# Gated-delta loop of a hybrid decoder trunk: eight heads a chunk at a time, against two groups of four heads half a chunk apart

## Chip, cores, metric

One core of one Trainium2 chip. The metric is device time in microseconds (us) of one launch; before: 3519.69 us, median of 3 runs (3516.3 to 3522.31). A difference of 0.2% is about what a measurement of this kernel can tell from none.

## What is computed

Two layers over 1024 tokens of width 1024, all in float32: layer 0 mixes with gated linear attention and an RG-LRU, layer 1 with a gated DeltaNet of 8 heads (key and value width 128); each layer then attends to 256 memory tokens and applies a squared-ReLU MLP. The change touches the gated DeltaNet's loop alone:

```python
L = jnp.exp(jnp.where(incl, gcum[..., :, None] - gcum[..., None, :], -jnp.inf))
M = jnp.where(strict, jnp.einsum('bhnid,bhnjd->bhnij', kb, kc) * L, 0.0)      # kb = k * beta
IM = M + jnp.eye(CHUNK, dtype=F32)
sol = lax.linalg.triangular_solve(IM, rhs, left_side=True, lower=True, unit_diagonal=True)
Aqk = jnp.where(incl, jnp.einsum('bhnid,bhnjd->bhnij', qc, kc) * L, 0.0)
def step(S, inp):                                       # one chunk, all heads
    v_new = un - jnp.einsum('bhcd,bhdv->bhcv', wn, S)
    o = jnp.einsum('bhcd,bhdv->bhcv', qn * jnp.exp(gn)[..., None], S) + jnp.einsum('bhij,bhjv->bhiv', an, v_new)
    S = S * jnp.exp(glast)[..., None, None] + jnp.einsum('bhcd,bhcv->bhdv', kn * jnp.exp(glast[..., None] - gn)[..., None], v_new)
    return S, o
```

q and k are divided by their l2 norms first; o goes through an RMS norm and is multiplied by a gate (silu(z)).

## The kernel before, in words

The program is written engine by engine; every engine has its own list in program order, and semaphores join them. Nothing is reordered by a planner inside the stage: the order is the order of the calls. Most of the kernel is projections (L1899 and L1915: each weight is split in two parts, three matmuls of 128x512 for one product), with weights streamed by SyncE.

The stage at issue works on 8 chunks of 128 tokens, 8 heads each, data of a chunk in units of 128x1024 (8 heads side by side, 4 heads in each of two PSUM banks). For chunk c+1 it **prepares**, for chunk c it **finishes**, and `both(c)` (one loop round) holds both; `prepare(0)` stands ahead of the loop, `finish(7)` behind it, among the first projections of the output (`out1`).

On TensorE, one round is, in this order:

- `state_keys` (ks, L2224: key times state), `start` (grow, L2234: the cumulated gate sent to all rows by 2 matmuls with ones; kt, L1953: keys transposed; nrm, L2241: squares of q and k summed by 16 matmuls with a column of ones), `new_values` (vn, L2224: inverse times right side), `keys_values` (knt and vt, L1953), `output_state` (o, L2267 and L2268; su, L2224), `matrices` (g and qk, L2224; z, L2285: seeds of the inverse).
- `inverse`: six levels. A level has, for each half k of the heads, `products` (q, L2299, at the last level L2302), 2 transposes of the inverse so far (t, L2334), then `updates` (x, L2313, at the last level L2316), all on 64x64 tiles of the array, 32 columns each. Between products and updates ScalarE copies both results to SBUF (L999 and L1003); after the updates VectorE merges them into the inverse (L1778), and the next level's products wait for it. The halves alternate. The output's transposes (ot, L1953) stand ahead of level 2.

A float32 matmul shows as two records in the trace, a transpose as one.

ScalarE also squares q and k (L958, L960), takes the norms' power (L962, L963), copies vn and knt (L967, L978), computes the decays' exponentials (L971 to L976), squares the output (L983) and issues the loads of q, k, v and the gate (L944, 4 a chunk). VectorE does the products of whole units: 128x1024 TENSOR_TENSORs L1695 to L1793. GpSimd does three products a chunk (L480, L482, L485).

Of the kernel before, what the change touches and what calls it, by code (L numbers as in the profile page):

```python
# [17 lines left out]
F32 = mybir.dt.float32  # L18
# [169 lines left out]
def build(nc, xT, memT, wstream, lru_w, gk_w2, pvec_in, consts_in, masks_in, outT):  # L188
# [4 lines left out]
    with ExitStack() as ctx:  # L193
# [79 lines left out]
        def every(ap, n):  # L273
# [43 lines left out]
        loaded = [sem(f"loaded_{k}") for k in "qkvz"]  # L317
# [3 lines left out]
        inv = range(LEVELS - 1)  # L321

        ppe = Steps(sem("gdn_prep_pe"), "grow kt nrm knt vt g qk z " +
                    " ".join(f"q{n}0 t{n}0 q{n}1 t{n}1 x{n}0 x{n}1" for n in inv))
        fpe = Steps(sem("gdn_fin_pe"), "ks vn o su ot")
        pact = Steps(sem("gdn_prep_act"), "sqk sqq rk eg L LT sc knt " +
                     " ".join(f"q{n}0 t{n}0 q{n}1 t{n}1" for n in inv) + " zd")
        fact = Steps(sem("gdn_fin_act"), "vn osq ro hi")
        ppool = Steps(sem("gdn_prep_pool"), "L qg kd")
        pdve = Steps(sem("gdn_prep_dve"), "dg m kn vb mn z beg at " +  # L330
                     " ".join(f"z{n}{k}" for n in inv for k in range(2)))
        fdve = Steps(sem("gdn_fin_dve"), "r o1 s ss o2 res lo")
# [19 lines left out]
        def in_lin(first, *shape):  # L352
            n = 1
            for k in shape:
# [19 lines left out]
        gs = {name: small[:, 128 + 8 * k:128 + 8 * k + n] for name, k, n in  # L374
              (("rkq", 0, 16), ("dec", 2, 8), ("gd", 3, 8), ("egl", 4, 8), ("gl", 5, 8), ("egt", 6, 8), ("g", 7, 8),
               ("ro", 8, 8), ("oss", 9, 8), ("nb", 10, 8), ("bt", 11, 8), ("beg", 12, 8), ("rqs", 13, 8), ("egs", 14, 8))}
# [10 lines left out]
        own = small[:, 248:312]  # L387
        Qc = unit(14)[:, 0:256].rearrange("p (t m n) -> p t m n", t=2, m=GDN_H // 2)
        Qt = unit(14)[:, 0:256].rearrange("p (m n) -> p m n", m=GDN_H // 2)
# [6 lines left out]
        def gdn_chunks(link, prepare, finish, both, per):  # L396

            prepare(0)
            link.loop(NCH - 2, per, lambda c: both(c, True))
            both(NCH - 2, False)  # L400
            finish(NCH - 1)
# [18 lines left out]
        def _(sp):  # L420
# [9 lines left out]
            for layer in range(2):  # L430
                n1 = plan.at[f"mlp{layer}.1"][0]
                for n in range(n, n1):
                    if n == plan.at["out0"][0] + 3:
                        sp.wait_ge(gpe.sem, gpe.at("tr", NCH - 1))
                    if n == plan.at["out1"][0] + 3:
                        sp.wait_ge(fpe.sem, fpe.at("su", NCH - 1))
# [17 lines left out]
        def _(pool):  # L454
# [22 lines left out]
            def gdn(p):  # L477
# [21 lines left out]
            with pool.Fori(0, NCH) as p:  # L499
                gdn(p)  # L500
# [3 lines left out]
        def _(eng):  # L504
# [378 lines left out]
            def mixer1():  # L883
# [63 lines left out]
                def loads(p):  # L947
# [3 lines left out]
                    for kind in (1, 0, 2):  # L951
                        load(kind, p)
# [1514 lines left out]
```

## Time and profile before

| what | before |
| --- | --- |
| median of 3 runs | 3519.69 us (3516.3 to 3522.31) |
| the profiled execution's own time | 3515.1 us |
| its span, first to last instruction | 3513.3 us |
| mean granted TensorE clock | 0.942 |
| TensorE busy | 3300.2 us, 94% of the span |
| VectorE, ScalarE, GpSimd busy | 1633.0, 1065.3, 155.2 us |
| DMA | 189.10 MB, mean 54 GB/s |

Busy time says little by itself: an engine that waits for a result between two short instructions is idle for a short time each, and TensorE is busy twice as long for the same work when its granted clock is 0.5 (1.2 GHz) and not 1.0 (2.4 GHz). Where the stage is bound has to be read from its own stretch.

### The profile page before, as it was taken

What the parts mean: (1) busy time and instruction counts of PE and PEld (TensorE: products, weight loads), DVE (VectorE), ACT (ScalarE), POOL (GpSimd) and SP (SyncE); (2) the same over time, 40 slices, a digit from 0 to 9 for tenths busy, and PEclk for the clock granted to TensorE, in tenths of its full rate; (3) what the DMA queues carried; (4) which work ended last, traced back from release to release, by engine and by line L of the source; (5) the groups of instructions that cost most, each with busy time, mean ns of one, the idle gap of its engine ahead of it and who ended that gap; (6) DMA issues with size and microseconds to landing.
All of it is one profiled execution on the core that took longest, in us unless ns stands there. A gap on an engine that the chain in (4) does not pass through costs nothing.

```text
span 3513.3 us, 45268 instructions
## 1 busy us (share of the span) xinstructions
PE 3300.2 (94%) x17926; PEld 2686.5 (76%) x17926; DVE 1633.0 (46%) x2171; ACT 1065.3 (30%) x1615; POOL 155.2 (4%) x270
## 2 busy tenths in 40 slices
PE   7996699989999999999999888899998999999997
PEld 6685588767788888877887677778876778888886
DVE  6264556436333333367555444544643543333335
ACT  3332344225222222233111333333432422222222
POOL 0005400000000000000000101100000000000000
PEclk9998899999999999999999677769999999999998
DMA  3010131101111111112222111113110111111112
GB/s 118 30 48 19 54 120 37 42 21 46 45 47 49 47 49 47 49 38 96 96 96 93 49 46 42 30 31 101 62 36 12 49 49 48 48 48 48 48 48 72
DMA packets 80223, 189.10 MB, mean 54 GB/s; under 512 B 5728, under 2 KB 38768, under 8 KB 79600
## 3 DMA queue, kind: packets, MB, share of 16 engines
q1 hardware_dynamic: 40320, 141.91, 12.4%
q10 hardware_dynamic: 39792, 45.63, 3.9%
q8 instruction: 79, 1.29, 0.1%
q14 instruction: 32, 0.26, 0.0%
HBM read 166.55 MB, written 20.97 MB: 53 GB/s over the span
## 4 chain that ended last, share of the span: by engine, by line
PE 82%; DVE 9%; ACT 4%; issue 3%; POOL 1%; DMA 1%; ACTq 0%; DVEq 0%; POOLq 0%; SPq 0%
PE ps L1899 52%; PE ps L1915 14%; PE ps L2046 2%; PE ps L2224 1%; PE ps L2026 1%; PE ps L2334 1%; DVE work L1116 1%; PE ps L1953 1%; PE ps L2313 1%; DVE hres L1147 1%; PE ps L2299 1%; DVE work L1132 1%; PE ps L2241 1%; DMA wraw<-wstream_dram 1%; ACT whi L520 1%
## 5 line engine op out<-in xcount | busy, mean ns | idle before, releaser
L1899 PE MATMUL ps<-act,whi 128*128 128x512 f32 x3712 | 1178.6, 399 | 33.9 <-DVE wlo L1100 18.3
L1899 PEld LDWEIGHTS ps<-act,whi 128*128 128x128 f32 x3712 | 702.2, 190 | 201.4 <-DVE wlo L1100 20.9
L1899 PE MATMUL ps<-act,wlo 128*128 128x512 f32 x1856 | 732.2, 395 | 0.0
L1899 PE MATMUL ps<-hid,whi 128*128 128x512 f32 x2048 | 637.5, 393 | 3.3 <-DVE work L1388 2.3
L520 ACT ACTIVATE whi<-wraw 128x1024 fp32r<-128x1024 f32 x262 | 276.4, 1058 | 924.1 <-DMA wraw<-wstream_dram 922.7
L1100 DVE TENSOR_TENSOR wlo<-wraw,whi 128x1024 fp32r<-128x1024 f32 x262 | 320.6, 1225 | 464.5 <-ACT whi L520 461.6
L1899 PEld LDWEIGHTS ps<-hid,whi 128*128 128x128 f32 x2048 | 384.2, 188 | 88.8 <-DVE wlo L1100 4.6
L1915 PE MATMUL ps<-act,whi 128*128 128x512 f32 x1536 | 416.3, 393 | 7.4 <-DVE work L1486 4.3
L1899 PEld LDWEIGHTS ps<-act,wlo 128*128 128x128 f32 x1856 | 352.2, 190 | 77.9
L1899 PE MATMUL ps<-hid,wlo 128*128 128x512 f32 x1024 | 398.1, 389 | 0.0
L1915 PEld LDWEIGHTS ps<-act,whi 128*128 128x128 f32 x1536 | 290.4, 189 | 72.2 <-issue 10.3
L1390 DVE TENSOR_TENSOR work<-work,ps 128x512 f32<-128x512 f32 x224 | 152.4, 686 | 277.4 <-PE ps L1899 277.4
L1915 PE MATMUL ps<-act,wlo 128*128 128x512 f32 x768 | 238.8, 392 | 0.0
L1899 PEld LDWEIGHTS ps<-hid,wlo 128*128 128x128 f32 x1024 | 192.3, 188 | 42.5
L1373 DVE SCALAR_TENSOR_TENSOR hidf<-ps,work 128x512 f32<-128x512 f32 x128 | 87.6, 687 | 242.7 <-PE ps L1899 236.7
L731 ACT ACTIVATE hidf<-hidf 128x512 f32<-128x512 f32 x128 | 80.9, 632 | 346.7 <-DVE hidf L1373 346.7
L1915 PEld LDWEIGHTS ps<-act,wlo 128*128 128x128 f32 x768 | 145.3, 189 | 31.3
L1176 DVE SCALAR_TENSOR_TENSOR work<-work,pvec 128x1023 f32<-128x1023 f32 (+2 forms) x84 | 107.8, 1283 | 8.0 <-DVE work L1172 0.2
L2224 PE MATMUL ps<-work 128*128 128x128 f32 x640 | 94.6, 316 | 5.7 <-DVE work L1781 5.7
L480 POOL TENSOR_TENSOR work<-work,small 128x1024 f32<-128x1024 f32 x8 | 15.2, 1898 | 1861.7 <-ACT work L972 1861.7
L2224 PEld LDWEIGHTS ps<-work 128*128 128x128 f32 x640 | 90.3, 228 | 7.3 <-DVE work L1781 5.2
L1116 DVE TENSOR_TENSOR work<-work,sq 128x512 f32<-128x512 f32 x84 | 57.8, 688 | 78.4 <-ACT sq L548 78.3
(274 smaller groups left out, 3271.7 us busy)
## 6 DMA issues: line engine op xcount, KB each, us to landing
wraw<-wstream_dram SPq DMA_DIRECT2D x262, 512.0 KB, 3.5
qkvz<-work ACTq DMA_DIRECT2D x32, 512.0 KB, 2.6
work<-qkvz ACTq DMA_DIRECT2D x32, 512.0 KB, 5.3
hres<-xT_dram ACTq DMA_DIRECT2D x8, 512.0 KB, 11.0
hres<-xT_dram ACTq DMA_DIRECT2D x1, 4096.0 KB, 12.2
outT_dram<-hres SPq DMA_DIRECT2D x16, 256.0 KB, 2.0
work<-memT_dram ACTq DMA_DIRECT2D x2, 1024.0 KB, 4.7
work<-masks_in_dram ACTq DMA_DIRECT2D x1, 1024.0 KB, 15.9
```

The lines of the kernel that those rows point to most:

```text
L520: A(whi[s][:], wraw[s][:], ACT.Copy).then_inc(w_hi, 1)
L731: link(A(hidf[:, t, 1, E[e]], hidf[:, t, 1, E[e]], ACT.Square))
L1100: TT(wlo[s][:], wraw[s][:], whi[s][:].bitcast(F32), ALU.subtract).then_inc(w_split, 1)
L1116: TT(uh(SSQ, e), uh(SSQ, e), sq[:] if src is None else src, ALU.add).then_inc(sq_used, 1)
L1132: STT(out=uh(t, e), in0=uh(t, e), scalar=col(post, k0 + t), in1=uh(RSTD, e), op0=ALU.mult, op1=ALU.mult).then_inc(normed_done, 1)
L1176: ins = STT(out=out[:, back:], in0=x[:, 0:SEQ - back], scalar=w(3 - back), in1=out[:, back:], op0=ALU.mult, op1=ALU.add)
L1373: STT(out=hidf[:, t, 1, E[e]], in0=out_of(u + k), scalar=0.0, in1=uh(RSTD, e), op0=ALU.max, op1=ALU.mult).then_inc(evac, 1)
L1390: TT(uh(t, e), uh(t, e), out_of(u + 8 + k), ALU.add).then_inc(evac, 1)
L1899: last = mm(out_of(u)[:, 0:width], (wlo if hl else whi)[s][:, at:at + P], rhs(kt, xp, e), start=kt == hl == xp == 0, stop=kt == kts - 1 an ...
L1915: last = mm(out_of(u)[:, E[e]], (wlo if hl else whi)[s][:, kt * P:(kt + 1) * P], act[:, kt, xp, E[e]], start=kt == hl == xp == 0, stop=kt ...
L2046: last = mm(bank(6 + d), v[:, m, at:at + P], pt[:, m * HALF:(m + 1) * HALF], start=m == 0, stop=m == 1)
L2224: last = mm(bank(first_bank + (h // 4 - hs[0] // 4))[:, (h % 4) * P:(h % 4 + 1) * P], lhs[:, h, :], rhs[:, h, :], start=start, stop=stop)
```

## The change

The heads are split into two groups g of four. The program goes in **slots**, two to a chunk: a slot holds the inverse of one group at one chunk, and between its products and its updates, and behind the updates, products of the other group: what finishes that group's older chunk (`fin`), prepares its next (`prep`), and, of the inverse's own group, the output's transposes of an older chunk (`old`) and `state_keys`. Each group has four PSUM banks of its own. There are 17 slots: the first only prepares, the last prepares nothing. Loads are by group: 8 a chunk, half as large.

Besides, the norms' squares are summed on ScalarE: three times four ACTIVATEs of 128x128 with `accum_out` a slot in place of two squares of 128x1024, 16 matmuls with a column of ones, the output's square and a TENSOR_REDUCE. The queries are now transposed too (4 more transposes a slot). The gate's row comes from 4 matmuls of 128x128 with a broadcast column. VectorE takes four 128x128 SCALAR_TENSOR_TENSORs with a per-head scalar in place of a TENSOR_TENSOR pair (`matrix`, `rhs`, `state`).

The order of the slots, and the ScalarE, VectorE and TensorE code of a slot:

```diff
+        def gdn_slots(link, slot, per):
+
+            slot(None, None, None, (0, 0))
+            slot((0, 0), None, None, (1, 0))
+            slot((1, 0), None, (0, 0), (0, 1))
+
+            def body(i):
+                slot((0, i + 1), (0, i), (1, i), (1, i + 1))
+                slot((1, i + 1), (1, i), (0, i + 1), (0, i + 2))
+            link.loop(NCH - 2, per, body)
+            slot((0, NCH - 1), (0, NCH - 2), (1, NCH - 2), (1, NCH - 1))
+            slot((1, NCH - 1), (1, NCH - 2), (0, NCH - 1), None)
...
+                def key_squares(g, p):
+                    eng.wait_ge(fdve[g].sem, fdve[g].at("sv", p - 1))
+                    eng.wait_ge(ppe[g].sem, ppe[g].at("kt", p))
+                    for k in range(4):
+                        A(hd(14, g)[:, k, :], gb(g, 1)[:, k * P:(k + 1) * P], ACT.Square,
+                          accum_out=gs[g]["rk"][:, k:k + 1])
...
+                    if inverse:
+                        level(*inverse, 0)
+                    if prep:
+                        key_squares(*prep)
+                    if fin:
+                        new_values(*fin)
+                    if inverse:
+                        level(*inverse, 1)
+                    if prep:
+                        query_squares(*prep)
+                        state_decay(*prep)
+                    if inverse and not (isinstance(inverse[1], int) and inverse[1] == NCH - 1):
+                        loads(inverse[0], inverse[1] + 1)
...
+                    if fin:
+                        output_squares(*fin)
+                    if inverse:
+                        level(*inverse, 4)
+                    if fin:
+                        output_rms(*fin)
+                    if prep:
+                        keys(*prep)
...
+                    if inverse:
+                        level(*inverse, 5)
+                    if fin:
+                        output_scaled(*fin)
+                    if inverse:
+                        next_scalars(*inverse)
+                        kept_scalars(*inverse)
+                    if prep:
+                        seed(*prep)
+                        scores(*prep)
...
+                def state_update(g, c, more=True):
+                    on(fact[g], "vn", c)
+                    on(ppool[g], "kd", c)
+                    if more:
+                        on(pact[g], "eg", c + 1)
+                    fpe[g].done(each(gb(g, 0), KD, VN, g), "su")
...
+                    ppe[g].done(last, f"t{n}")
+                    between()
+                    on(pact[g], f"t{n}", p)
+                    met()
+                    ppe[g].done(updates(g, n), f"x{n}")
...
+                    at = [raw, transposed, half, turned_values, lambda: state_keys(*inverse), scored]
                     for n in inv:
...
+                        if inverse:
+                            level(*inverse, n, at[n])
+                        elif n != 4:
+                            at[n]()
+                        if n == 0 and fin:
+                            new_values(*fin)
+                        if n == 1 and fin:
+                            state_update(*fin, more=prep)
+                        if n == 2 and fin:
+                            output(*fin, 2)
+                        if n == 3 and prep:
+                            keys(*prep)
+                        if n == 4 and prep:
+                            gram(*prep)
+                    if prep:
+                        seed(*prep)
```

A slot on TensorE begins with `decays(*prep)` (grow). Between products and updates of levels 0 to 5 stand: the transposes of raw keys and queries (8), of the output (4), the first half of o, the transposes of the values (4), ks, qk. Behind the updates of levels 0 to 4: vn, su, the second half of o, knt, g. The seeds z of the next inverse come last. What the lines left out of ScalarE's slot do: behind level 2 the norms' Ln and Exp, the copy to the result's high part and the decay's Exp, behind level 3 one small Exp ahead of `output_squares`.

**How the rows move.** TensorE before, level 1 of the inverse (`work` holds the units, `consts` the identity); both halves of the heads, nothing else between:

```order
L2299 MATMUL ps<-work 64x32 [waits gdn_prep_dve]
L2299 MATMUL ps<-work 64x32 x7
L2334 MATMUL ps<-consts,work 128x128 x2
L2299 MATMUL ps<-work 64x32 [waits gdn_prep_dve]
L2299 MATMUL ps<-work 64x32 x7
L2334 MATMUL ps<-consts,work 128x128 x2
L2313 MATMUL ps<-work 64x32 [waits gdn_prep_act]
L2313 MATMUL ps<-work 64x32 x7
L2313 MATMUL ps<-work 64x32 [waits gdn_prep_act]
L2313 MATMUL ps<-work 64x32 x7
```

Of the change, levels 1 and 2 of a slot (L2367 products, L2396 transposes, L2381 updates; L2277 the output's transposes, L2272 state update, both of other steps):

```order
L2367 MATMUL ps<-work 64x32 [waits gdn_prep_dve0]
L2367 MATMUL ps<-work 64x32 x7
L2396 MATMUL ps<-consts,work 128x128 x2
L2277 MATMUL ps<-consts,work 128x128 [waits gdn_fin_dve0]
L2277 MATMUL ps<-consts,work 128x128 x3
L2381 MATMUL ps<-sq,work 64x32 [waits gdn_prep_act0]
L2381 MATMUL ps<-sq,work 64x32 x7
L2272 MATMUL ps<-work 128x128 [waits gdn_prep_act1,gdn_prep_pool1,gdn_fin_act1]
L2272 MATMUL ps<-work 128x128 x3
L2367 MATMUL ps<-work 64x32 [waits gdn_prep_dve0]
L2367 MATMUL ps<-work 64x32 x7
```

A level is 8 products, 2 transposes and 8 updates of one group, and other work now stands both ahead of the updates (L2277) and behind them (L2272, which waits for ScalarE and GpSimd).

TensorE at the end of the last slot but one, behind the loop (L2384 last updates, L2323 seeds, L2272 scores; inside the loop grow, L2288, stands between seeds and products):

```order
L2272 MATMUL ps<-work 128x128 [waits gdn_prep_dve1]
L2272 MATMUL ps<-work 128x128 x3
L2384 MATMUL ps<-sq,work 64x64 [waits gdn_prep_act0]
L2384 MATMUL ps<-sq,work 64x64 x3
L2323 MATMUL ps<-consts,work 64x64 [waits gdn_fin_dve1,gdn_prep_dve1]
L2323 MATMUL ps<-consts,work 64x64 x7
L2367 MATMUL ps<-work 64x32 [waits gdn_prep_dve1]
L2367 MATMUL ps<-work 64x32 x7
L2396 MATMUL ps<-consts,work 128x128 [waits gdn_prep_dve1]
```

The seeds wait for VectorE's matrix and state, and the next level 0 for VectorE's merge of the seeds.

ScalarE of the change, levels 0 and 1 of a slot (L1037 and L1040 the two copies of a level, L981 and L987 squares with sums, L1014 new values, L1000 the state's decay):

```order
L1037 ACTIVATE sq<-ps 128x128 [waits gdn_prep_pe0]
L1040 ACTIVATE work<-ps 128x256 [waits gdn_prep_pe0]
L981 ACTIVATE work,small<-ps 128x128 [waits gdn_prep_pe1,gdn_fin_dve1]
L981 ACTIVATE work,small<-ps 128x128 x3
L1014 ACTIVATE work<-ps 128x512 [waits gdn_fin_pe1]
L1037 ACTIVATE sq<-ps 128x128 [waits gdn_prep_pe0]
L1040 ACTIVATE work<-ps 128x256 [waits gdn_prep_pe0]
L987 ACTIVATE work,small<-ps 128x128 [waits gdn_prep_pe1]
L987 ACTIVATE work,small<-ps 128x128 x3
L1000 ACTIVATE work<-ps 128x512 [waits gdn_prep_dve1,gdn_prep_pool1,act_chain]
```

Eight squares, a copy and an exponential of the other group now stand between the copies of one level and those of the next; `L1000` (eg, for which the state update waits) stands behind eight squares.

## Rows read from the trace of the kernel before

**Rows 1.** The page of before: span and granted clock in 40 slices.
```profile
span 3513.3 us, 45268 instructions
PEclk9998899999999999999999677769999999999998
```

**Rows 2.** Stretches: us, busy PE, PEld, DVE, ACT, POOL, then PEclk, DMA share, GB/s.
```profile
1934.70:2367.40 432.70, 381.54 (x4633) 316.78 (x4633) 208.48 (x404) 159.46 (x334) 52.58 (x24) 0.70 0.15 39
2310.67:2364.40 53.73, 48.62 (x590) 40.24 (x591) 26.98 (x51) 20.73 (x43) 6.71 (x3) 0.72 0.04 11
2316.80:2340.70 23.90, 20.49 (x232) 19.30 (x232) 14.79 (x17) 8.09 (x15) 6.71 (x3) 1.00 0.00 1
2340.70:2364.40 23.70, 22.00 (x350) 16.36 (x347) 8.08 (x27) 10.52 (x27) 0.00 (x0) 0.50 0.01 2
2081.20:2088.10 6.90, 5.61 (x166) 4.13 (x158) 2.81 (x11) 4.45 (x12) 0.00 (x0) 0.99 0.00 0
```

**Rows 3.** Timeline (start us, us, engine, line): stage begin, products at 1.2 GHz, out1 begins.
```profile
1934.71 3.54 PE L2234 MATMUL ps<-work,consts 128*128 128x512 f32 x4 [6.39 <-DVE work L1695]
2310.67 3.75 PE L2224 MATMUL ps<-work 128*128 128x128 f32 x16 [0.78 <-DVE work L1781]
2367.38 0.98 PE L1899 MATMUL ps<-act,whi 128*128 128x512 f32 x2
```

**Rows 4.** Timeline of one inverse level of both halves at 1.2 GHz.
```profile
2347.42 0.65 PE L2299 MATMUL ps<-work 64*64 64x32 f32 x16
2349.82 1.41 PE L2313 MATMUL ps<-work 64*64 64x32 f32 x32
2351.16 0.65 PE L2299 MATMUL ps<-work 64*64 64x32 f32 x16
```

**Rows 5.** Timeline, TensorE at 2.4 GHz: transposes, products, seeds, a level with its releases.
```profile
2323.74 1.97 PE L1953 MATMUL ps<-consts,work 128*128 128x128 f32 x16
2329.12 5.52 PE L2224 MATMUL ps<-work 128*128 128x128 f32 x48
2334.57 1.15 PE L2285 MATMUL ps<-consts,work 64*64 64x64 f32 x32
2339.43 0.44 PE L2334 MATMUL ps<-consts,work 128*128 128x128 f32 x2 [2.19 <-DVE work L1758]
2339.79 0.43 PE L2299 MATMUL ps<-work 64*64 64x32 f32 x16
2340.16 0.44 PE L2334 MATMUL ps<-consts,work 128*128 128x128 f32 x2
2340.69 0.38 ACT L1003 ACTIVATE work<-ps 128x256 f32<-128x256 f32 x1
2340.53 1.35 PE L2313 MATMUL ps<-work 64*64 64x32 f32 x32
2341.26 0.45 DVE L1778 COPY_PREDICATED work<-masks,ps 128x64 f32<-128x64 uint8 x2 [1.89 <-PE ps L2313]
```

**Rows 6.** Groups by line and form (count, busy us, mean ns, idle before), whole run or stage.
```profile
L1390 DVE TENSOR_TENSOR work<-work,ps 128x512 f32<-128x512 f32 x224 | 152.4, 686 | 277.4 <-PE ps L1899 277.4
L1579 DVE SCALAR_TENSOR_TENSOR lin<-lin,small,ps 128x128 f32<-128x128 f32 x16 | 4.8, 344 | 36.0 <-PE ps L2182 36.0
L731 ACT ACTIVATE hidf<-hidf 128x512 f32<-128x512 f32 x128 | 80.9, 632 | 346.7 <-DVE hidf L1373 346.7
L1003 ACT ACTIVATE work<-ps 128x256 f32<-128x256 f32 x96 | 36.9, 384 | 44.0 <-PE ps L2334 42.0
L2241 PE MATMUL ps<-consts,work 128*128 128x1 f32 x256 | 30.5, 253 | 0.0
```

**Rows 7.** Timeline of ScalarE: an accumulating ACTIVATE twice in a row.
```profile
611.01 0.47 ACT L673 ACTIVATE work<-ps,small 128x256 f32<-128x256 f32 x1 [2.16 <-DVE small L1282]
611.48 0.47 ACT L673 ACTIVATE work<-ps,small 128x256 f32<-128x256 f32 x1
```

**Rows 8.** One source line, the loads that ScalarE issues: ns min, median, max.
```profile
L944 ACTq DMA_DIRECT2D work<-qkvz x32: 374/473/2872, 1931.3 to 2363.7; - x32
```

More of the change, by code:

```diff
@@ L1796, in prepare @@
[L1796 to L1831 removed]
+                    on_pe(ppe[g], f"x{n}", p)
@@ new lines, in level, with rhs, next_scalars @@
+                    pdve[g].done(copy, f"z{n}")
+                def rhs(g, c):
+                    on_pe(fpe[g], "ks", c)
+                    for k in range(4):
+                        last = STT(out=hd(9, g)[:, k, :], in0=gb(g, 3)[:, k * P:(k + 1) * P],
+                                   scalar=gs[g]["nbeg"][:, k:k + 1], in1=hd(9, g)[:, k, :], op0=ALU.mult, op1=ALU.add)
+                    fdve[g].done(last, "r")
+                def next_scalars(g, c):
+                    fdve[g].done(scalars(g, c if isinstance(c, int) and c == NCH - 1 else c + 1), "st")
@@ new lines, in turned, with decays @@
+                def turned(out, src, g):
+                    for h in H[g]:
+                        last = tr(out[:, (h % 4) * P:(h % 4 + 1) * P], src[:, h, :], ident)
+                    return last
+                def decays(g, p):
+                    if isinstance(p, int) and p == 0:
+                        eng.wait_ge(gdn_first, g + 1)
+                    else:
+                        on(fdve[g], "st", p - 1)
+                    on(pdve[g], f"z{LEVELS - 2}", p - 1)
+                    for k in range(4):
+                        last = mm(gb(g, 0)[:, k * P:(k + 1) * P], gs[g]["g"][:, k:k + 1].to_broadcast([P, P]), ident,
+                                  start=True, stop=True)
+                    ppe[g].done(last, "grow")
@@ L2288, in output_transposes @@
[L2288 to L2295 removed]
+                    if first:
+                        fpe[g].done(last, "o")
+                def output_transposes(g, c):
+                    on(fdve[g], "o2", c)
+                    fpe[g].done(turned(gb(g, 3), heads(19), g), "ot")
@@ L2296, in products, with updates @@
+                def updates(g, n):
+                    lv = LEVELS - 2 - n
+                    for m in range(2):
                         for t, (r, at) in enumerate(T64):
@@ new lines, in mixer1 @@
+                gdn_slots(link, slot, 0)
+                n, u = plan.at["out1"]
+                output_transposes(0, NCH - 1)
+                new_values(1, NCH - 1)
+                for g in range(2):
+                    on(fdve[g], "lo", NCH // 2 - 1)
+                on(fdve[0], "res", NCH - 1)
+                units([(n, u)], 0)
+                state_update(1, NCH - 1, more=False)
+                output(1, NCH - 1, 0)
+                output(1, NCH - 1, 2)
+                units([(n + 1, u + 1)], 0)
@@ L2375, in _ @@
+                units([(n + 2, u + 2)], 0)
+                output_transposes(1, NCH - 1)
+                units([(n + 3, u + 3)], 0)
+                for g in range(2):
+                    on(fdve[g], "lo", NCH - 1)
+                for k in range(4):
+                    units([(n + k, u + 4 + k)], 1, after={3: lambda: mem_stat_(1)} if k == 0 else None)
+            for s in (gpe, *ppe, *fpe):
                 s.credit(eng)
```

714 lines of the change are left out of this document (328 added, 386 removed).

## The prediction

> **What bounds the kernel now.** I read the page first: a span of 3513.3 us with a granted clock of 9 and 10 tenths nearly everywhere, but 6 and 7 tenths in the slices that hold the gated-delta loop [rows 1]. Then the stage by stretches: from the first grow product to the first product of out1 it takes 432.7 us, TensorE is busy for 381.5 of them, every other engine for less than half, at a mean clock of 0.70 [rows 2, 3]. So TensorE bounds the stage, and half of the reason is its clock. One chunk takes 53.73 us. Its products run for 23.9 us at clock 1.00, then the inverse for 23.7 at 0.50, where TensorE still counts as busy for 22.0 [rows 2]. The clock fell at 2340.7, 4 us after the products had given way to the inverse, and rose at 2316.8, 6 us after the next chunk's products had begun (ks, 3.75 us at the slow clock [rows 3]). A level of the inverse for all eight heads takes 3.74 us at 1.2 GHz (L2299 from 2347.42 to 2351.16 [rows 4]).
>
> **The change, part by part.** All sums are at 2.4 GHz first; the clock comes after.
>
> *Prices.* A 128-column record costs 5.52/48 = 0.115 us, so a product of four heads (8 records) 0.92; a transpose 1.97/16 = 0.123; the 8 products of a level 0.37 until the next record (2339.79 to 2340.16); 16 seed matmuls 1.15, so 8 cost 0.58 [rows 5]. ScalarE's copy of 128x256 is 0.384 and an ACTIVATE of 128x512 0.632; VectorE's 128x512 0.686, its scalar_tensor_tensor of 128x128 0.344 [rows 6]. A loads' issue holds ScalarE for 0.473 [rows 8]. No row shows a 128x128 square with a sum. Bounds: at 128x256 one such follows the next after 0.47 [rows 7]; without the sum 128x128 costs no less than 0.25 (0.384 less 128 elements' share). I take 0.345: 0.47 less those 0.13.
>
> *The chain of one level*, if nothing else stood in the queues: products 0.37, from the transposes' start to ScalarE's second copy 0.53 (2340.16 to 2340.69), the copy 0.38, to the updates 0.12, updates to VectorE's merge 0.73 (2340.53 to 2341.26), the merge 0.45, and 0.11 to the next products [rows 5]: 2.7 us. Before, the two halves of the heads fill it for each other; now the other group's products do.
>
> *A slot, level by level.* Ahead of the updates TensorE has 0.37 + 0.25 and the work put between, or the 1.4 of the chain if that is longer; behind them 0.35 and the work put there, or the remaining 1.3.
> - Level 0: 8 transposes between, vn behind: 1.6 + 0.35 + 0.92 = 2.9.
> - Level 1: 4 transposes are hidden. Behind the updates stands su, and su waits for eg, which ScalarE runs behind the level's copies and four squares: 1.3 + 4 x 0.345 + 0.63 + 0.13 = 3.4, then su 0.92: 4.3. This is a wait of 1.7 us that the change adds, and level 2 is queued behind it.
> - Level 2: both halves of o, 0.62 + 0.92 + 0.35 + 0.92 = 2.8.
> - Level 3: little to fill with (0.5 each side), the chain sets it: 2.7.
> - Level 4: ks between; g behind the updates waits for ScalarE's copy of knt, which stands behind the level's copies and the output's Ln and Exp: 1.3 + 0.45 + 0.63 + 0.13 = 2.5, then g 0.92: 3.4, less 0.1 of overlap: 3.3.
> - Level 5 and the end: qk between, 1.54, updates 0.35, then the next slot's grow waits until VectorE has merged (0.2 + 0.55), scaled the output (0.16 + 0.69) and copied three small tiles (0.3): 1.9; to grow 0.13, grow 0.92. Sum 4.8. Seeds (0.58) fit in that wait.
>
> The sum is 20.8 us; 0.2 more for waits and registers, of which a slot has some twenty beside a half chunk's ten: 21.0, so 42.0 a chunk against 53.7. TensorE's own work in a slot is 64 records (7.4), 32 transposes (3.9), seeds (0.6), five levels of 32 small records (3.7) and the last (0.6): 16.2. ScalarE's is 12 squares (4.1), five of 128x512 (3.2), six levels' copies (4.0), the inverse's diagonal (0.8), small ones (0.8) and 4 issues (1.9): 14.8. VectorE's is about 14. None of them fills 21 us: the orders and waits between them do.
>
> *What goes:* the 32 one-column records, 30.5/8 = 3.8 us a chunk [rows 6], go from TensorE; 4 transposes a group (0.5) and ScalarE's squares come. It is in the sums above. Loads are hidden: they are issued half a chunk or more ahead and are the same bytes.
>
> *The stage.* Slot 0 (no inverse, partly at 1.2 GHz) 15, slots 1 to 15 at 21.0: 315, slot 16 (no preparation) 19, to out1's first product 5: 354 us. Before: 432.7. The rest of out1 keeps its length (it ends in the same wait for the last low parts). So 78.7 come off. From the profiled execution's own 3515.1 this gives 3436.4; its time lies 4.6 below the median of 3519.7, from which I count: **3441 us**.
>
> *The clock, which decides.* I take 2.4 GHz in the slots because 128-column products, which went at 1.00 in the product half, now stand in every level, and TensorE's pauses are short (at most 1.9 us at a slot's end). Even the inverse alone once ran at 0.99 for 6.9 us (2081.2 to 2088.1 [rows 2]). Against it: the clock fell at 2340.7 although TensorE's longest pause ahead of it was 2.19 us [rows 5], little more than the 1.9 of a slot's end.
> The Trainium skill (TensorE: Matmul & The Clock Gate, "Why this matters for your kernels") advises to leave no long idle gap between bursts of matmuls, and by that alone the whole stage would hold 2.4 GHz, so 354 us; but this trace disagrees as to the inverse, where the pauses were short and the clock fell nevertheless. The same page (Part 4) says that transposes don't count as busy for the clock, which speaks against this change, as it has 64 transposes a chunk; no stretch here shows it apart.
>
> **The rivals.**
> 1. *The clock stays at 1.2 GHz* (slower). If mixed slots don't lift it, a slot is TensorE's work at the slow clock: 64 x 0.234 (3.75/16 [rows 3]) = 15.0, transposes 7.9, seeds and last level 2.4, small records 160 x 0.042 (1.34/32 [rows 4]) = 6.7, sum 32.0. Stage: 20 + 15 x 32 + 28 + 6 = 534, that is 101 slower: 3621 us. For it: half of each chunk runs so today. Against it: ks at the slow clock was enough to lift it at 2316.8 before any other work. The change turns slower where a slot costs over 26.2 us (432.7 less the 39 of the other slots, over 15), which is with about half of the slots' time at 1.2 GHz.
> 2. *The clock comes and goes.* The thin places (level 3, level 1's wait, the slot's end) let it fall, and it returns some us later. With a quarter of the time at 1.2 GHz a slot is 21.0 + 0.25 x 11 = 23.8: 45 us of the gain go, 3486. The alternation of the chunks before speaks for it. By the page's rule on transposes this case becomes likelier, with the same price.
> 3. *ScalarE's queue decides more.* If a square costs its upper bound of 0.47, levels 0 and 1 and those with output squares grow: 12 x 0.125 = 1.5 a slot, 24 us in all: 3465. The in-order copies behind them make this likely to be paid in full.
> 4. *The change doesn't do what it says:* TensorE, in order, waits with its filler in hand. That is what levels 1 and 4 above show, 1.7 and 1.1 us a slot; if every filler waited so, a slot would be 25 and the time 3505.
>
> **Numbers.** Forecast (clock held, 20 to 22 us a slot) 0.66: 3441, alone 3420 to 3460. Rival 3 0.12, rival 2 0.13, rival 4 0.03, rival 1 0.06. The range of 3415 to 3490 leaves out rival 1, rival 4 and the tails, 2 in 10 at most; its low end is a slot of 19.5, by the square's lower bound and smaller waits. 0.2% of the time (7 us) is what a measurement can tell from none. Faster by more: 0.93; within: 0.01; slower: 0.06.
>
> **What would show it.** Stage from first grow to first out1 near 354 us; starts of successive slots (the first square of keys) 21 us apart; PEclk 1.00 between; in a slot, su waiting for ScalarE's `work` some 1.5 us, g for about 1, grow for VectorE's `small` nearly 2. Squares 0.35 apart. I am wrong if the clock in the stage reads under 0.85, or if slots are over 23 us at clock 1.00, or if another stage changes its length by over 5 us.

## The result and the profile after

The change takes 3435.49 us (median of 4 runs, 3424.54 to 3437.15) beside 3520.79 for the kernel before (median of 4, 3516.3 to 3522.31): ratio 0.9753, 95% interval 0.973 to 0.9776. Predicted were 3441 us, 3415 to 3490. The profiled execution took 3437.15 us.

| what | before | after |
| --- | --- | --- |
| profiled execution's own time | 3515.1 us | 3437.15 us |
| TensorE busy | 3300.2 us | 3221.5 us |
| VectorE, ScalarE, GpSimd busy | 1633.0, 1065.3, 155.2 | 1604.4, 1096.1, 158.8 |
| stage, first grow to first product of out1 | 432.7 us | 358.8 us |
| mean granted clock in the stage | 0.70 | 0.93 |
| half a chunk, or one slot | 26.9 us | 20.9 us |

The page after, to be held against [rows 1]: the slices at 6 and 7 tenths are gone.

```profile
span 3435.4 us, 45556 instructions
...
PE   7997699999999999998999888889998999999997
PEclk9998799999999999999999899999999999999998
```

The stretches of the stage after (us, then busy time of PE, PEld, DVE, ACT, POOL, then PEclk, DMA share, GB/s), against [rows 2]: the stage; five slots in a row without a fall of the clock; one with a fall; a single slot.

```profile
1939.30:2298.10 358.80, 302.01 (x4581) 259.73 (x4581) 189.40 (x619) 189.85 (x758) 56.25 (x48) 0.93 0.17 48
2000.00:2104.25 104.25, 89.70 (x1440) 77.17 (x1441) 59.35 (x196) 59.64 (x240) 17.55 (x15) 1.00 0.18 51
2104.25:2126.55 22.30, 19.43 (x288) 16.78 (x289) 11.54 (x41) 11.90 (x48) 3.55 (x3) 0.92 0.16 47
2062.55:2083.37 20.82, 17.95 (x289) 15.45 (x289) 11.85 (x41) 11.90 (x48) 3.51 (x3) 1.00 0.18 50
```

TensorE's busy time in the stage fell from 381.5 to 302.0 us, and VectorE and ScalarE work for 53% of it each. A slot is 20.8 us at clock 1.00. In two of the twelve slots from 2000 to 2253 us the clock falls for 3.4 us, and such a slot takes 22.3 to 22.4; ahead of them, in the first slots, it is still low at times.

One slot on TensorE (timeline: start us, us, engine, line; L2367 and L2370 are the products with which a level starts, L2272, of which the lines of vn, su and g are shown, in this order, and L2288 the next slot's gate row), against [rows 4, 5]:

```profile
2084.45 0.43 PE L2367 MATMUL ps<-work 64*64 64x32 f32 x16
...
2086.42 1.16 PE L2272 MATMUL ps<-work 128*128 128x128 f32 x8
2087.51 0.43 PE L2367 MATMUL ps<-work 64*64 64x32 f32 x16
...
2090.61 1.16 PE L2272 MATMUL ps<-work 128*128 128x128 f32 x8 [1.29 <-ACT work L1000]
2091.70 0.43 PE L2367 MATMUL ps<-work 64*64 64x32 f32 x16
...
2094.78 0.43 PE L2367 MATMUL ps<-work 64*64 64x32 f32 x16
...
2097.25 0.43 PE L2367 MATMUL ps<-work 64*64 64x32 f32 x16
...
2099.44 1.16 PE L2272 MATMUL ps<-work 128*128 128x128 f32 x8
2100.53 0.45 PE L2370 MATMUL ps<-work 64*64 64x64 f32 x8
...
2104.25 1.15 PE L2288 MATMUL ps<-consts,small 128*128 128x128 f32 x8 [1.18 <-DVE small L1738]
2105.34 0.43 PE L2367 MATMUL ps<-work 64*64 64x32 f32 x16
```

The levels start 3.06, 4.19, 3.08, 2.47, 3.28 and 4.81 us apart. Two waits stand in the slot: 1.29 us of su for ScalarE's exponential, 1.18 us of the gate row for VectorE's small copy. What is ahead of each on its engine (ScalarE, then VectorE; the second line of ScalarE is the reading of a square's sum):

```profile
2088.63 0.27 ACT L987 ACTIVATE work<-ps 128x128 f32<-128x128 f32 x1
2088.79 0.20 ACT L987 ACTIVATION_READ_ACCUMULATOR work<-ps 128x1 f32 x1
2088.88 0.28 ACT L987 ACTIVATE work<-ps 128x128 f32<-128x128 f32 x1
...
2089.96 0.60 ACT L1000 ACTIVATE work<-ps 128x512 f32<-128x512 f32 x1 [0.19 <-ACT work L987]
2090.27 1.50 ACTq L967 DMA_DIRECT2D work<-qkvz  x3
```

```profile
2103.36 0.69 DVE L1829 TENSOR_TENSOR work<-ps,small 128x512 f32<-128x512 f32 x1
2103.97 0.15 DVE L1738 COPY small<-small 128x12 f32 x1
```

The query's squares stand ahead of L1000, 0.25 us apart; the scaling of the output (L1829) stands ahead of L1738, the copy that the gate row needs. Summed over the stage, these are the two largest waits of TensorE (by line and form: count, busy us, mean ns, idle before and its releasers), against [rows 6]; the third line is the output's square on ScalarE, which comes up further down:

```profile
L2272 PE MATMUL ps<-work 128*128 128x128 f32 x632 | 93.4, 294 | 19.9 <-ACT work L1000 17.5 <-ACT work L1010 0.7
L2288 PE MATMUL ps<-consts,small 128*128 128x128 f32 x128 | 20.0, 303 | 20.4 <-DVE small L1738 20.4
L1019 ACT ACTIVATE work<-ps,small 128x128 f32<-128x128 f32 x60 | 21.1, 370 | 0.0
```

### The profile page after: what moved, and what is told of

Its sections match the earlier page's. It is cut to its first block, busy times and chain, and to the rows that moved or that the text cites. A ratio compares the mean times of both kernels' runs of the same rounds, so it can differ in the third digit from the quotient of the medians.

```text
span 3435.4 us, 45556 instructions
## 1 busy us (share of the span) xinstructions
PE 3221.5 (94%) x17830; PEld 2628.9 (77%) x17830; DVE 1604.4 (47%) x2378; ACT 1096.1 (32%) x2047; POOL 158.8 (5%) x294
## 4 chain that ended last, share of the span: by engine, by line
PE 82%; DVE 8%; ACT 5%; issue 3%; DMA 1%; POOL 1%; DVEq 0%; ACTq 0%; SPq 0%; POOLq 0%
PE ps L1945 53%; PE ps L1961 15%; PE ps L2272 2%; PE ps L2092 2%; PE ps L2072 1%; DVE work L1166 1%; DVE hres L1197 1%; PE ps L2277 1%; DVE work L1182 1%; DMA wraw<-wstream_dram 1%; PE ps L2396 1%; DVE lin L1622 1%; ACT whi L543 1%; PE ps L2367 1%; PE ps L1973 1%
## 5 line engine op out<-in xcount | busy, mean ns | idle before, releaser
L2272 PE MATMUL ps<-work 128*128 128x128 f32 x640 | 94.5, 294 | 19.9 <-ACT work L1000 17.5
L502 POOL TENSOR_TENSOR work<-work,consts 128x512 f32<-128x512 f32 x16 | 20.3, 1272 | 1801.0 <-ACT work L1003 1801.0
L2272 PEld LDWEIGHTS ps<-work 128*128 128x128 f32 x640 | 82.7, 202 | 24.2 <-ACT work L1000 16.4
L1797 DVE COPY_PREDICATED work<-masks,ps 128x64 f32<-128x64 uint8 x160 | 30.1, 240 | 140.5 <-PE ps L2381 140.3
```

The costliest lines, as they stand in the source:

```text
L2272: last = mm(out[:, (h % 4) * P:(h % 4 + 1) * P], lhs[:, h, :], rhs[:, h, :], start=start, stop=stop)
```

## Experiments

The table has each kernel's stage, from the first grow product to the first of out1, read in one execution each; times are medians, ratios are to runs of before taken beside each (medians 3520.19 to 3520.83 us).

| kernel | median us | ratio, 95% interval | stage us | clock in it |
| --- | --- | --- | --- | --- |
| before | 3520.79 | | 432.7 | 0.70 |
| added matmuls in the inverse | 3511.89 | 0.9978 [0.9965, 0.9991] | 420.7 | 0.82 |
| added transposes in the inverse | 3502.99 | 0.9941 [0.992, 0.9963] | 424.6 | 0.78 |
| twice as many matmuls | 3511.36 | 0.9977 [0.9964, 0.9989] | 437.3 | 0.81 |
| the same, norms on ScalarE | 3534.68 | 1.0034 [1.0017, 1.0051] | 453.4 | 0.81 |
| norms on ScalarE alone | 3539.69 | 1.0058 [1.0038, 1.0077] | 455.4 | 0.68 |
| the change, groups apart | 3682.97 | 1.0453 [1.0436, 1.047] | 608.0 | 0.67 |
| groups apart, added matmuls | 3615.62 | 1.0286 [1.0255, 1.0317] | 537.3 | 0.91 |
| the change, fillers behind | 3471.82 | 0.9876 [0.9842, 0.9911] | 397.3 | 0.90 |
| the change | 3435.49 | 0.9753 [0.973, 0.9776] | 358.8 | 0.93 |
| the change, slot end reordered | 3418.87 | 0.9712 [0.9699, 0.9725] | 343.3 | 0.95 |
| the change, loads split | 3405.49 | 0.9677 [0.9664, 0.969] | 335.2 | 0.94 |
| both reorderings | 3393.62 | 0.9643 [0.963, 0.9656] | 324.5 | 0.94 |

**Before, with matmuls added in the inverse.** Is it the clock that makes the inverse slow, and can other work hold it?

```diff
                             ppe.done(updates(n, k), f"x{n}{k}")
+                            mm(bank(4)[:, 256:384], ident, consts[:, 0:128], start=True, stop=True)
```

> Before, with one added 128x128 float32 matmul (identity times identity, into PSUM columns that nobody reads) behind each half's updates of every inverse level: 12 a chunk, 24 records, 2.8 us of extra TensorE work a chunk at 2.4 GHz, 5.6 at 1.2 GHz. It adds work that the result doesn't need. My theory (the low clock of the inverse, not its waits alone, is a large part of the 53.7 us chunk, and 128-column matmuls among the small ones hold 2.4 GHz): granted clock in the inverse over 0.9, chunk 45 to 48 us, run about 50 us faster than before (3470). Rival (small 32-column matmuls with pauses keep the clock at 1.2 GHz whatever stands among them): clock stays 0.5 in the inverse, chunk 57 to 59 us, run 25 to 45 us slower (3545 to 3565).

**The same with transposes.**

```diff
                             ppe.done(updates(n, k), f"x{n}{k}")
+                            for o in (256, 384):
+                                tr(bank(4)[:, o:o + P], ident, ident)
```

> As the kernel with added matmuls, but with two 128x128 transposes (one record each, the same TensorE time) in the place of each added matmul. It adds work that the result doesn't need. If transposes lift and hold the clock as matmuls do: the same time within 5 us as with matmuls, about 3470. If transposes don't count as work for the clock (the Trainium skill, TensorE: Matmul & The Clock Gate, Part 4, says so): clock 0.5 in the inverse as before and 24 transposes of 0.24 us more a chunk, partly hidden in waits, so 25 to 45 us slower than before (3545 to 3565).

Both came out between theory and rival. A chunk of each (stretches, columns as above):

```profile
2200.80:2252.00 51.20, 47.20 (x614) 40.00 (x612) 27.36 (x52) 20.01 (x42) 6.63 (x3) 0.87 0.15 41
```

```profile
2211.00:2262.30 51.30, 47.16 (x615) 38.96 (x613) 27.35 (x52) 20.01 (x42) 6.63 (x3) 0.83 0.15 41
```

With matmuls the clock is 0.87 in a chunk of 51.2 us. It falls after the pauses of 1.25 and 2.37 us in which TensorE waits for VectorE's seeds and scores, stays down for 10.2 us, and is 1.00 for the last four levels. The same level at both clocks (L2299 begins a level):

```profile
2138.11 0.43 PE L2299 MATMUL ps<-work 64*64 64x32 f32 x16
...
2141.19 0.43 PE L2299 MATMUL ps<-work 64*64 64x32 f32 x16
...
2179.40 0.65 PE L2299 MATMUL ps<-work 64*64 64x32 f32 x16
...
2184.28 1.91 PE L1953 MATMUL ps<-consts,work 128*128 128x128 f32 x8
```

3.08 us at 2.4 GHz (2138.11 to 2141.19) and 4.88 at 1.2 (2179.40 to 2184.28, where transposes of another step follow), both without a wait. So the first expectation was right that other work lifts the clock in the inverse, and wrong that it would hold it there throughout: it left out the pauses at the inverse's start. The time falls by 9 us only, because the additions cost most of what the clock gives. Transposes do the same: clock 0.83 in a chunk of 51.3, and the run was 9 us shorter again by the medians, though not in the execution profiled (3512.13 us beside 3507.61). The rule that transposes don't count as work for the clock (the Trainium skill, TensorE: Matmul & The Clock Gate, Part 4) would have given a clock as before and 3545 or more; here the measurement disagrees: among small matmuls added transposes lift the clock from 0.70 to 0.78 over the stage, matmuls in their place to 0.82.

**Before, the pause at level 0 filled too.** One matmul stays behind each half's updates, as above; these twelve come on top.

```diff
+                    for _ in range(4):
+                        mm(bank(6)[:, 0:P], ident, ident, start=True, stop=True)
                     for n in inv:
...
                             ppe.done(products(n, k), f"q{n}{k}")
                             if n == 0 and k == 0:
+                                for _ in range(8):
+                                    mm(bank(6)[:, 0:P], ident, ident, start=True, stop=True)
```

> Before, with one added 128x128 float32 matmul behind each half's updates (as in the first filling kernel, where the clock still fell for 13.6 of the 51.2 us of a chunk, from the pause of 1.25 and 2.37 us in which TensorE waits for VectorE's seeds and scores at level 0), and 12 more of them in that pause: 24 a chunk, 5.5 us of work that the result doesn't need. My theory (the clock falls in that pause, and the inverse then cannot lift it): clock 1.00 throughout but for some 3 us a chunk behind the 32 one-column records, an inverse level of 3.1 us, chunk 46.5 to 48, run 40 to 50 us faster than before (3470 to 3480). Rival (the small matmuls bring it down wherever they stand): clock 0.5 for 10 us or more a chunk as before, chunk 51 to 54, run within 20 us of before.

**The same with the norms on ScalarE.**

```diff
-                    on(pact, "sqq", p)
-                    for k, t in enumerate((7, 14)):
-                        for h in range(GDN_H):
-                            last = mm(bank(4)[:, 8 * k + h:8 * k + h + 1], heads(t)[:, h, :], ones[:, 0:1], start=True,
-                                      stop=True)
-                    ppe.done(last, "nrm")
+                    eng.wait_ge(loaded[0], 16 * p + 16)
+                    ppe.done(transposes(heads_of(bank(4, 2)), heads(0), GDN_H), "nrm")
```

> The same added matmuls, and the norms as in the changed kernel: squares of q and k by head on ScalarE with their sum, 8 transposes of q in the place of 32 one-column records. If the one-column records are what lets the clock fall for 3.4 us a chunk: clock 1.00, chunk 44.5 to 47, run 3450 to 3470. With it the chunk of before is known at 2.4 GHz: if it is within 4 us of the 41.8 of the change, the clock is most of the gain; if it is over 48 although the clock is 1.00, the filled waits are.

Both expectations were missed in time, and the first was right for some chunks only. Two chunks in a row of the first kernel:

```profile
2159.50:2208.60 49.10, 46.17 (x638) 39.76 (x636) 27.35 (x52) 20.01 (x42) 6.63 (x3) 0.97 0.16 42
2208.60:2269.60 61.00, 58.47 (x639) 49.31 (x638) 27.78 (x53) 20.90 (x43) 6.63 (x3) 0.72 0.16 42
```

The same instructions take 49.1 us at clock 0.97 and 61.0 at 0.72: 11.9 us by the clock, as the waits are the same within 0.4 us. In the second, TensorE is busy for 58.5 of 61.0 us, and the clock stays at 1.2 GHz for 27.3 us in a row all the same. What that is worth to the kernel before, without additions, its own trace shows in the one stretch in which its inverse ran at 2.4 GHz (in [rows 2], 2081.20 to 2088.10):

```profile
2082.83 0.43 PE L2299 MATMUL ps<-work 64*64 64x32 f32 x16
...
2085.41 0.43 PE L2299 MATMUL ps<-work 64*64 64x32 f32 x16
```

A level takes 2.58 us there, against 3.74 at 1.2 GHz [rows 4]: 7.0 us for six levels. From the start of ks to the transposes behind grow 6.5 us pass in a chunk of before (2310.67 to 2317.21), mostly at the slow clock, and 3.7 in the held chunk (2157.59 to 2161.29): another 2.8. So a chunk of before at 2.4 GHz is estimated at 53.7 - 9.8 = 43.9 us.

The held chunk gives a second estimate. The twelve matmuls added at level 0 lie in pauses and cost it only 0.35 us: from the seeds to the second transposes of level 0 it takes 5.21 us, and before 4.86 (2334.57 to 2339.43 in [rows 5]). The other twelve lengthen a level from 2.58 to 3.08 us (2194.03 to 2197.11 in this chunk), so 3.0 over six levels.

```profile
2180.11 1.15 PE L2285 MATMUL ps<-consts,work 64*64 64x64 f32 x32
...
2185.32 0.44 PE L2338 MATMUL ps<-consts,work 128*128 128x128 f32 x2 [0.39 <-DVE work L1758]
```

49.1 less these 3.35 is 45.8, and 44.2 without the 1.6 that one fall of the clock costs vn and knt in that chunk. The change takes 41.7. So of the 12 us a chunk that it gains, the clock makes 8 to 10 by these estimates, and 2 to 4 are left for all the rest.

With the norms moved as well, chunks alternate between 51.3 and 61.2 us, the quicker ones 1 to 2 us longer than the quick ones without, and the run is 23 us longer. The 3.4 us falls did not go away, so the one-column records were not their only cause. This kernel was to show a chunk at clock 1.00 and with it the clock's share; the quick chunks ran at 0.93, so that question was not settled by it.

**Before, the norms alone.** The part of the change that takes the 32 one-column records away.

```diff
-                    pact.done(A(unit(7), unit(1), ACT.Square), "sqk", p)
...
+                    eng.wait_ge(ppe.sem, ppe.at("kt", p))
+                    for h in range(GDN_H):
+                        last = A(heads(7)[:, h, :], bank(2, 2)[:, h * P:(h + 1) * P], ACT.Square,
+                                 accum_out=gs["rkq"][:, h:h + 1])
```

> Before, with that part of the change alone: the norms' squares of q and k by head on ScalarE with their sum, 8 transposes in the place of 32 one-column records, nothing added. On TensorE 3.8 us a chunk go and 1.0 come; ScalarE does 16 squares of 0.25 us where it did two of 1.2, and it is waited for there. My theory: 0 to 2 us a chunk, run 0 to 15 us faster (3505 to 3520). Rival (the 3.8 us come off in full): 3490 to 3495. If ScalarE's sums cost more than their squares saved: up to 10 us slower.

It was slower, by 19 us, more than even the third case said. A chunk takes 57.7 us at clock 0.68. TensorE and ScalarE in it (L1958 transposes, L2229 vn, L959 and L964 the first of eight squares each, L968 the norms' last step):

```profile
2220.46 1.91 PE L1958 MATMUL ps<-consts,work 128*128 128x128 f32 x16
...
2221.53 0.28 ACT L959 ACTIVATE work<-ps 128x128 f32<-128x128 f32 x1 [7.48 <-PE ps L1958]
...
2222.20 1.95 PE L2229 MATMUL ps<-work 128*128 128x128 f32 x16
...
2223.95 0.28 ACT L964 ACTIVATE work<-ps 128x128 f32<-128x128 f32 x1
...
2226.50 0.21 ACT L968 ACTIVATE small<-small 128x16 f32<-128x16 f32 x1
...
2228.02 3.68 PE L1958 MATMUL ps<-consts,work 128*128 128x128 f32 x16 [3.87 <-DVE work L1720]
```

The squares no longer start from the loaded data while ks and grow run; they wait for transposes. The 3.8 us of records became a wait of 3.87, and the normalized keys are transposed 10.2 us after grow has begun (2217.85 to 2228.02), not 9.5. The clock fell in this wait (0.50 from 2226.5 to 2233.3), so that from there to su it took 7.9 us and not 5.4 (2323.74 to 2329.12 in [rows 5]). In the slots the squares stand between an inverse's copies. They are not free there either: four of them, 1.0 us, stand ahead of the exponential for which su waits 1.29. No run takes them out of the slots, so what they cost in all is open.

**The change, groups apart.** The same slots and the same instructions, but the other group's work first and then six levels with nothing between, on TensorE, ScalarE and VectorE.

```diff
-                            level(*inverse, n, at[n])
...
+                    if inverse:
+                        state_keys(*inverse)
+                        for n in inv:
+                            level(*inverse, n, lambda: None)
```

> The change with its two groups, its sums on ScalarE and its slots, but nothing between: in each slot all work of the other group first and then the six levels of the inverse bare, on TensorE, ScalarE and VectorE. My theory (the gain comes from the other group's work in the gaps of the chain): six bare levels of 2.7 us (more at 1.2 GHz) plus some 14 us of other work and its waits, a slot of 30 to 36 us, the stage 490 to 580 us, so 60 to 150 us slower than before and about 3580 to 3660. Rival (the gain comes from the removed one-column matmuls, smaller operations and four banks a group, not from the order): slot under 24 us and under 3490.

**The same, with matmuls added behind the updates.**

```diff
                     ppe[g].done(updates(g, n), f"x{n}")
+                    for o in (256, 384, 256):
+                        mm(gb(g, 2)[:, o:o + P], ident, ident, start=True, stop=True)
```

> The groups apart (nothing between in the inverse), with three 128x128 float32 matmuls added behind each level's updates, 18 a slot, 4.1 us at 2.4 GHz of work that the result doesn't need, in a gap of 1.3 us a level. If the clock is then held at 2.4 GHz: a level of 2.7 to 2.9 us, slot 28 to 31 us in the place of 37.6, run 105 to 150 us faster than without them (3530 to 3580); the rest to the 20.9 of the change is what filled gaps give at an equal clock. If the clock still falls (rival): a slot of 38 to 41, run 0 to 50 us slower than without them.

Groups apart took 3683 us, slots of 37.6, somewhat more than expected; with the additions 3616, slots of 31.2 at clock 1.00, but the clock fell in others, so that 67 us came off and not 105. A slot of each:

```profile
2174.40:2212.10 37.70, 25.72 (x289) 21.90 (x289) 12.52 (x40) 12.42 (x48) 3.55 (x3) 0.68 0.10 29
```

```profile
2144.10:2175.30 31.20, 23.24 (x326) 19.84 (x325) 13.63 (x40) 12.36 (x48) 3.95 (x3) 1.00 0.13 37
```

A bare level took 2.56 us at 2.4 GHz (3.16 at 1.2), with additions 2.60: the chain of one group, which nothing shortens. At an equal clock a slot is 31.2 with the groups apart and 20.8 woven: 10.4 us is what weaving is worth against this order, in which su and g also wait 2.07 and 1.77 us for ScalarE. 6.5 more is the clock that it holds (37.7 less 31.2, with 18 added matmuls that cost a level 0.04 us). The rival (smaller operations and four banks a group do it) falls: without the weaving the change is 162 us slower than before.

**The change, fillers behind the updates only.**

```diff
                     ppe[g].done(last, f"t{n}")
-                    between()
                     on(pact[g], f"t{n}", p)
                     met()
                     ppe[g].done(updates(g, n), f"x{n}")
+                    between()
```

> The change, but on TensorE alone the work that stands between a level's products and its updates is put behind the updates, ahead of what stands there already. ScalarE's and VectorE's order is unchanged. My theory (both gaps of a level, the 1.4 us up to the updates and the 1.3 us behind them, have to be filled): levels 0 to 5 of 3.7, 4.5, 3.6, 2.8, 3.7, 5.3 us, slot 23.5 instead of 20.9, run about 40 us slower than the change (3475). Rival (TensorE's order inside a level doesn't matter, as its work just has to fit in the slot): within 8 us of the change.

3471.82 us, as expected, but for another reason in part. Slots alternate:

```profile
2087.40:2110.00 22.60, 18.50 (x293) 15.52 (x289) 11.91 (x40) 11.92 (x48) 3.51 (x3) 1.00 0.16 48
2110.00:2135.20 25.20, 21.18 (x290) 17.88 (x288) 11.86 (x39) 11.90 (x48) 3.55 (x3) 0.86 0.14 41
```

Each level now waits 0.56 us ahead of its updates for ScalarE's copy, 3.4 us a slot. Half of that comes back, since the gate row waits no more and su only 0.70: 22.6 us, not 23.5. The other 2.6 us of every second slot are a fall of the clock of 6.8 us.

**The two waits of the change.** First the gate row's: VectorE's slot end.

```diff
-                    if fin:
-                        output_scaled(*fin)
                     if inverse:
                         next_scalars(*inverse)
-                        kept_scalars(*inverse)
                     if prep:
                         seed(*prep)
                         scores(*prep)
+                    if inverse:
+                        kept_scalars(*inverse)
+                    if fin:
+                        output_scaled(*fin)
```

> The change with VectorE's slot end in another order: the three small copies for which the next slot's gate row waits come right behind the last merge, then the seeds' merge and the scores, and the scaling of the output last. My theory (that row waits 1.18 us a slot for the small copies, which stand behind the scaling, and nobody needs the scaled output before level 1 of the next slot): the wait goes, the slot is 19.7 to 20.2 us in the place of 20.9, 11 to 19 us over 16 slots: run 3416 to 3425. Rival (the seeds' merge is late next, so that the first products wait in the gate row's place): slot within 0.2 us, run within 5 us of the change's 3435.

Then su's, on ScalarE; the loads of q and v go behind level 4's copies.

```diff
-                        query_squares(*prep)
                         state_decay(*prep)
+                        query_squares(*prep)
...
-                    for kind in (1, 0, 2):
-                        load(kind, g, p)
+                    load(1, g, p)
```

> The change with ScalarE's level 1 in another order: the state's decay exponential ahead of the four query squares, only the key load issued there, and the loads of q and v issued behind level 4's copies, where ScalarE waits. My theory (the state update waits 1.29 us a slot for that exponential, which stands behind four squares of 0.25): the wait goes, slot 19.7 to 20.2, run 3416 to 3425. Rival (the copies of level 2, behind the same squares, are late next): slot 20.4 to 20.8, run 3427 to 3434.

And both.

> Both reorderings together. If the two waits are separate: slot 18.5 to 19.2, run 3400 to 3410. Rival by the clock: TensorE's pauses are shorter, so its clock should fall less often than the twice in 16 slots of the change, not more; if it falls more often, the gain is under 15 us.

TensorE's waits ahead of the same two lines as in the change (there 19.9 and 20.4 us over the sixteen slots of the stage), here from 1960 to 2290 us, in which fourteen gate rows stand; slot end reordered, loads split, both:

```profile
L2273 PE MATMUL ps<-work 128*128 128x128 f32 x624 | 91.0, 291 | 19.2 <-ACT work L1000 17.5
L2289 PE MATMUL ps<-consts,small 128*128 128x128 f32 x112 | 16.1, 287 | 5.3 <-DVE small L1738 5.3
```

```profile
L2277 PE MATMUL ps<-work 128*128 128x128 f32 x624 | 90.5, 290 | 1.8
L2293 PE MATMUL ps<-consts,small 128*128 128x128 f32 x112 | 16.1, 287 | 15.6 <-DVE small L1743 15.6
```

```profile
L2278 PE MATMUL ps<-work 128*128 128x128 f32 x624 | 90.3, 289 | 1.8
L2294 PE MATMUL ps<-consts,small 128*128 128x128 f32 x112 | 16.1, 287 | 5.3 <-DVE small L1743 5.3
```

Each edit takes most of its own wait and leaves the other. The slot is 20.0, 19.6 and 18.8 us. Reordering the slot end was worth what was expected. Splitting the loads gave more: 3405 in the place of 3416 to 3425, 30.0 us below the change, of which 23.6 lie in the stage: 1.3 a slot, the two falls of the clock, and a clock that was up sooner in slots 1 and 2. In both kernels without su's wait the clock didn't fall in the steady slots; with the loads split:

```profile
1964.20:2244.00 279.80, 255.34 (x4113) 220.12 (x4112) 169.00 (x562) 165.71 (x676) 49.10 (x42) 1.00 0.18 53
```

The reordered kernel that keeps su's wait had three falls, the change two. All five begin where that wait ends: from 0.1 us ahead of su's start to 1.4 behind it. One of them, where the products run at 1.2 GHz from 2120.90 us on:

```profile
2120.74 1.96 PE L2273 MATMUL ps<-work 128*128 128x128 f32 x8 [1.29 <-ACT work L1000]
```

Both edits together make 3393.62 us, 42 below the change and 127 below the kernel before.

## Why the prediction was right

- **What bounds the stage.** TensorE, and half of it the clock: right. The share of the clock was not worked out in the prediction; it is estimated above at 8 to 10 of 12 us a chunk. The reading of why it rose at 2316.8 was incomplete: not ks alone, grow too had run ahead of it, from 2314.22 on.
- **The slot.** 21.0 predicted, 20.8 to 20.9 found; levels 2.9, 4.3, 2.8, 2.7, 3.3, 4.8 against 3.06, 4.19, 3.08, 2.47, 3.28, 4.81. The chain of a level, taken as 2.7, was 2.47 to 2.60.
- **The waits inside it.** su 1.7 us, found 1.29; the gate row 1.9 with the seeds in it, found 1.7, of which 1.18 is a pause; g about 1, found 0.2. All three were taken too long, su's by about what four squares were priced too high (0.38), and the level times were right nevertheless, by errors that cancel: a product of four heads, taken as 0.92, occupies TensorE for 0.99 to 1.09 us before the next shape starts (2090.61 to 2091.70), and level 4 is full with ks, updates and g.
- **The square with a sum.** Taken as 0.345, bounds 0.25 and 0.47: 0.25 for q and k, the lower bound. With a scale by row (the output's, L1019) one took 0.370, and they follow each other at 0.34 to 0.35. The reading of the accumulator (0.2 us, a row of its own) lies under the next square. Rival 3 falls with it.
- **The clock.** It held, with 48 us at 1.2 GHz in the stage in the place of 259. The reason given was right in part: with 128-column work between the small products it held in ten of twelve slots, but with two pauses of 1.2 to 1.3 us a slot it fell in two, and without su's it held for 280 us.
- **The stage.** 354 predicted, 358.8 found. Slots 1 and 2 took 22.0 and 23.6 at clocks 0.74 and 0.86 (3.6 more than 42), the two falls cost 3.0, and a slot of 20.8 in the place of 21.0 saved some 2.0 over twelve.
- **Behind the stage.** "The rest of out1 keeps its length" was wrong: from its first product to ScalarE's next split of weights (2416.9 before, 2341.2 after), 49.5 us became 43.1. On TensorE only one group's su, o and output transposes stand in it now (28 records, before 72 with both groups' and vn), and a wait of 1.11 us ahead of o is gone; the rest went into the last slots and to just ahead of out1. These 6.4 us, and 2.3 further behind, stand against the 4.8 of the stage and against a stage that began 4.6 us later in that execution, over code that the change doesn't touch. So 3436.4, said of the profiled execution, met 3437.15 by errors that cancel in part.
- **Rival 2** (the clock comes and goes) is what the first slots and the two falls show in little. Of the thin places that it named, level 1's wait is the one that goes with the falls: without it they are gone from the steady slots, and without the slot end's wait they are not, in one profiled execution of each kernel. **Rivals 1 and 4** fall; the groups apart show how they would have looked (clock 0.68, slots of 37.6).

Open is why the clock falls in some slots and not in others with the same instructions, and what a chunk of before takes at 2.4 GHz throughout, which no kernel here showed: 43.9 is put together from a level and two products, 44.2 to 45.8 from a chunk with additions.

## What to carry to other kernels

Where TensorE works through a chain of small products and the granted clock in that stretch is 0.5, first compare one step of the chain at both clocks in the trace: that is what other work between the steps can give, and adding useless work there shows it but gave little time back (9 to 18 us here). Weave real work of another group in, then move the two or three instructions for which TensorE waits once a round: each such wait costs its length and perhaps a fall of the clock. A part of a change that goes well inside the woven order (here the norms on ScalarE) can cost 19 us alone, so parts are judged in the order in which they will run.

## What the runs showed of the hardware

- The same instructions, from level 2 on without a wait between them, ran on at either clock. In the kernel with 24 additions a chunk, levels at 2.4 GHz kept it to the chunk's end, and in the next chunk levels at 1.2 GHz, with TensorE busy for 58.5 of 61.0 us, kept that for 27.3 us. Busy time doesn't tell which it will be.
- A pause alone doesn't tell either. In the slow one of those two chunks the clock fell within a wait of 1.88 us at level 1; in the held one it stayed over a wait of 1.97 us at the same place. The updates behind that wait, in the held chunk and in the slow one:

```profile
2191.49 0.43 PE L2313 MATMUL ps<-work 64*64 64x32 f32 x16 [1.97 <-ACT work L1003]
...
2242.17 0.65 PE L2313 MATMUL ps<-work 64*64 64x32 f32 x16 [1.88 <-ACT work L1003]
```

- Transposes among small matmuls lifted the clock nearly as matmuls of the same time did (0.78 and 0.82 over the stage, from 0.70).
- Half the clock did not double the time of everything. A 128-column record took 0.115 us at 2.4 GHz and 0.234 at 1.2 [rows 5, 3], but 16 small records were busy for 0.43 and 0.65 [rows 5, 4], and a level took 2.58 and 3.74. So the sentence ahead of the prediction that TensorE is busy twice as long at 0.5 holds for the large products alone.
